# The second layer's up product by seven products of halves, with the three convolution taps made on ScalarE and added on VectorE one unit later

## The reference

```python
D_FF, CONV_W = 2816, 3

def conv_ffn(h, w_up, conv_w, conv_b, w_down):
    u = h @ w_up                                   # (1, 256, 1024) @ (1024, 5632)
    u = lax.conv_general_dilated(u, conv_w[:, None, :], window_strides=(1,),
                                 padding=[(CONV_W // 2, CONV_W // 2)],
                                 dimension_numbers=("NWC", "WIO", "NWC"),
                                 feature_group_count=u.shape[-1]) + conv_b
    a, g = jnp.split(u, 2, axis=-1)
    return (jax.nn.silu(g) * a) @ w_down
```

## Time and profile before

| | us |
|---|---|
| median of 3 runs | 3460.23 |
| lowest and highest | 3457.03, 3462.57 |
| the profiled execution, its whole time | 3458.15 |
| its span in the profile | 3456.3 |
| PE busy in it | 3286.9 (95%) |
| mean granted clock of PE | 0.964 of full speed |

### The profile page before, as it was taken

One profiled execution on the slowest core, in us unless ns is written; L12 is line 12 of the kernel. 1 busy time (PEld: TensorE's weight loads), 2 busy tenths in 40 slices (PEclk: granted clock), 3 DMA queues, 4 the chain that ended last, 5 costly groups with the idle time before them and its releaser, 6 DMA issues.

```text
span 3456.3 us, 81384 instructions
## 1 busy us (share of the span) xinstructions
PE 3286.9 (95%) x34930; PEld 2812.1 (81%) x34931; DVE 864.6 (25%) x1957; ACT 687.8 (20%) x1501; POOL 431.8 (12%) x393
## 2 busy tenths in 40 slices
PE   7999789999999999999999999988999999999998
PEld 5886678884587788787799887778899999988888
DVE  2324745550122321114233113130000100011001
ACT  2324132221113422112211021201111211110011
POOL 1210125550021010000057010000000000000000
PEclk9999689999999999999999999988999999999999
DMA  6546012222223244343344443237999999944477
GB/s 274 196 165 232 3 49 86 85 74 75 82 92 115 92 158 137 126 140 109 110 159 159 157 138 106 95 125 314 370 380 400 400 383 378 399 161 154 140 272 292
DMA packets 94776, 637.79 MB, mean 185 GB/s; under 512 B 10784, under 2 KB 11824, under 8 KB 38592
## 3 DMA queue, kind: packets, MB, share of 16 engines
q1 hardware_dynamic: 92048, 627.58, 48.8%
q0 software_dynamic: 2608, 8.49, 0.8%
HBM read 634.97 MB, written 1.05 MB: 184 GB/s over the span
## 4 chain that ended last, share of the span: by engine, by line
PE 89%; DMA 4%; DVE 3%; ACT 2%; issue 2%; POOL 0%; SPq 0%; DVEq 0%; ACTq 0%
PE bank L994 18%; PE bank L608 18%; PE bank L666 16%; PE bank L563 13%; PE bank L687 5%; PE bank L579 5%; DMA ring<-in_moe_down 3%; PE bank L954 2%; PE bank L511 2%; PE bank L537 1%; PE bank L1009 1%; PE bank L723 1%; PE bank L705 1%; PE bank L712 1%; DMA ring<-in_moe_up 1%
## 5 line engine op out<-in xcount | busy, mean ns | idle before, releaser
L666 PE MATMUL bank<-PROJ,ring 128*64 128x80 f32 (+2 forms) x7776 | 636.2, 272 | 11.9 <-DMA ring<-in_moe_down 8.8
L666 PEld LDWEIGHTS bank<-PROJ,ring 128*64 128x64 f32 (+1 forms) x7776 | 508.7, 147 | 137.6 <-issue 90.2
L994 PE MATMUL bank<-MIX,ring 128*64 128x80 f32 x12544 | 471.9, 234 | 19.8 <-issue 9.5
L994 PEld LDWEIGHTS bank<-MIX,ring 128*64 128x64 f32 x12544 | 446.6, 137 | 45.9 <-issue 38.3
L563 PE MATMUL bank<-H,ring 128*128 128x256 f32 x1856 | 408.2, 383 | 3.3 <-ACT H L1175 3.3
L563 PEld LDWEIGHTS bank<-H,ring 128*128 128x128 f32 x1856 | 355.0, 192 | 56.1 <-issue 4.7
L994 PE MATMUL bank<-H,ring 128*128 128x256 f32 x896 | 193.7, 379 | 0.0
L608 PE MATMUL bank<-H,ring 128*64 128x128 f32 (+1 forms) x1296 | 185.2, 331 | 5.5 <-ACT H L1175 4.8
L994 PEld LDWEIGHTS bank<-H,ring 128*128 128x128 f32 x896 | 170.2, 190 | 23.4 <-issue 0.3
L608 PE MATMUL bank<-MIX,ring 128*64 128x128 f32 (+1 forms) x1272 | 181.2, 321 | 0.8 <-DVE MIX L1748 0.8
L687 PE MATMUL bank<-H,ring 128*128 128x256 f32 x768 | 178.0, 389 | 3.9 <-ACT PROJ L1264 3.7
(11 more groups left out here) (345 smaller groups left out, 3440.8 us busy)
## 6 DMA issues: line engine op xcount, KB each, us to landing
ring<-in_moe_up SPq DMA_DIRECT2D x224, 1024.0 KB, 7.2
ring<-in_moe_down SPq DMA_DIRECT2D x128, 896.0 KB, 6.4
ring<-in_up SPq DMA_DIRECT2D x44, 1024.0 KB, 4.8
ring<-in_mod_b SPq DMA_DIRECT2D x40, 1024.0 KB, 5.6
ring<-in_tproj SPq DMA_DIRECT2D x32, 1024.0 KB, 4.9
ring<-in_proj SPq DMA_DIRECT2D x26, 1024.0 KB, 4.8
ring<-in_gates SPq DMA_DIRECT2D x24, 1024.0 KB, 4.8
ring<-in_down SPq DMA_DIRECT2D x32, 704.0 KB, 4.0
```

Source lines behind the costliest of these rows:

```text
L666: mm = pe.matmul(B[bank][lo:lo + m, 0:width], w[:, k, lo:lo + m], src(s * half + k), start=s == 0 and k == 0, stop=s == 1 and k == half - 1)
L994: mm = pe.matmul(B[(t0 + 2 * j + t) % 4][lo:lo + m, 0:n], w[:, k, t * P + lo:t * P + lo + m], src[:, k, 0:n], start=k == 0, stop=k == KT - 1)
```

## The change

`up1` is added to the table `SEVEN` with a width of 256. PE runs `seven("up1", ...)`: `seven_unit` for each of the 22 units in place of 16 plain products. The ring, the order of the loads and the down product stay.

- POOL: `w_sums` for units 0 and 1 when `wout1` is finished, then `sums_ahead` for each unit. It no longer multiplies `a` and `g` in `up1`.
- DVE: `x_sums` after the norm, `c_sums` for each unit. The outer taps are no longer scalar_tensor_tensor on PSUM but four tensor_tensor additions of finished taps (`add`, new lines 1852 and 1857), one unit late; the product of `a` and `g` (`gated`, new line 1862) comes here, two units late. All inputs of these five lie in SBUF.
- ACT: the copy of the first product; three taps for each of the two tiles, all read from Y (`taps`, new lines 1253 and 1255); Silu one unit late (new line 1261). The middle tap goes to SC, the outer ones to the right half of X, which is free in this layer.

```diff
-SEVEN = ('proj0', 'wout0', 'up0', 'proj1', 'swup')
+SEVEN = ('proj0', 'wout0', 'up0', 'proj1', 'up1', 'swup')
...
+        def tap(j, t, w):
+            return CONV[:, j % 2, t, 0:T] if w == 1 else X[:, 4 * (j % 2) + w + t, T:TC]
...
-            pairs("up1", T, ("norm6_out", 0, 1))
+            seven("up1", "norm6_out")
```

ScalarE, `conv_taps` (for each unit: `head(j + 1)`, which copies the first product, then `step_of(j)`):

```diff
+                def taps(j, it):
+                    act.wait_ge(S("ffn_hid"), it * NSLOT + (FT + j + 1))
+                    for t in range(2):
+                        src = flat(seven_parts("up1", j)[0][:, 2 * t:2 * t + 2, :])
+                        col = lambda w: cw[:, bass.ds(it * (4 * NSLOT) + 4 * (t * FT + j) + w, 1)]
+                        act.activation(tap(j, t, 1), src, ACT.Identity, bias=col(3), scale=col(1))
+                        for w in (0, 2):
+                            ins = act.activation(tap(j, t, w), src, ACT.Copy, scale=col(w))
+                    ins.then_inc(S("conv_c"), 1)
+
+                def silu(j, it):
+                    act.wait_ge(S("conv_d"), it * NSLOT + (FT + j + 1))
+                    g = tap(j, 1, 1)
+                    act.activation(g, g, ACT.Silu).then_inc(lin_free, 2)
+
+                def step_of(j, it):
+                    seven_done("up1", j, it)
+                    if j > 0:
+                        silu(j - 1, it)
+                    taps(j, it)
```

VectorE, `conv_taps`:

```diff
+                def add(j, it):
+                    dve.wait_ge(S("conv_c"), it * NSLOT + (FT + j + 1))
+                    for t in range(2):
+                        o = tap(j, t, 1)[:, 1:T]
+                        ins = dve.tensor_tensor(o, o, tap(j, t, 0)[:, 0:T - 1], ALU.add)
+                    ins.then_inc(S("conv_l"), 1)
+                    dve.wait_ge(S("conv_l"), it * NSLOT + (FT + j + 1))
+                    for t in range(2):
+                        o = tap(j, t, 1)[:, 0:T - 1]
+                        ins = dve.tensor_tensor(o, o, tap(j, t, 2)[:, 1:T], ALU.add)
+                    ins.then_inc(S("conv_d"), 1)
+
+                def gated(j, it):
+                    dve.wait_ge(lin_free, it * (2 * NSLOT) + (t0 + 2 * j + 2 + 4))
+                    dve.tensor_tensor(PROJ[:, bass.ds(it * (NSLOT * T) + j * T, T)], tap(j, 0, 1), tap(j, 1, 1), ALU.mult)\
+                       .then_inc(S("ffn_hid"), 1)
...
+                        c_sums("up1", j, it)
+                        add(j - 1, it)
+                        gated(j - 2, it)
...
+            x_sums("up1", "norm6_out")
```

GpSimd:

```diff
-            conv_ffn(1, T)
+            pool.wait_ge(unit_done, base["wout1"] + 4)
+            w_sums("up1", 0)
+            w_sums("up1", 1)
+            with pool.Fori(0, FT // NSLOT) as it:
+                for j in range(NSLOT):
+                    sums_ahead("up1", j, it)
```

More of the change, by code:

```diff
@@ L28 @@
 MOD_A = 8
-SEVEN = ('proj0', 'wout0', 'up0', 'proj1', 'swup')
-SEVEN_UNITS = {'proj0': 11, 'wout0': 4, 'up0': 22, 'proj1': 4, 'swup': 22}
-SEVEN_WIDTH = {'proj0': 512, 'wout0': 512, 'up0': 512, 'proj1': 512, 'swup': 256}
+SEVEN = ('proj0', 'wout0', 'up0', 'proj1', 'up1', 'swup')
+SEVEN_UNITS = {'proj0': 11, 'wout0': 4, 'up0': 22, 'proj1': 4, 'up1': 22, 'swup': 22}
+SEVEN_WIDTH = {'proj0': 512, 'wout0': 512, 'up0': 512, 'proj1': 512, 'up1': 256, 'swup': 256}
 MOD_P = 22
@@ L409, in seven_parts @@
             n, q = SEVEN_WIDTH[name] // 2, seven_at(name) + j
-            if name in ("up0", "swup"):
+            if name in ("up0", "up1", "swup"):
                 at = 6 * T * (q % 2)
@@ L1249, in conv_ffn, with conv_taps, head @@
                     pair(j, 0)
+            def conv_taps():
+                cw = W("conv1", 2 * FT * 4)
+                def head(j, it):
+                    seven_head("up1", j, it)
+                def taps(j, it):
[16 more added lines that the diff above has]
+                    taps(j, it)
+                peel = FT % NSLOT
+                head(0, 0)
+                for j in range(peel):
+                    head(j + 1, 0)
+                    step_of(j, 0)
+                with act.Fori(0, FT // NSLOT - 1) as it:
+                    for j in range(peel, peel + NSLOT):
+                        head(j + 1, it)
+                        step_of(j, it)
+                for j in range(FT - NSLOT, FT):
+                    if j + 1 < FT:
+                        head(j + 1, 0)
+                    step_of(j, 0)
+                silu(FT - 1, 0)
             def mod_row(n):
@@ L1818, in conv_ffn, with conv_taps @@
                     pair(j, 0)
+            def conv_taps():
+                t0 = tile_base["up1"]
+                def add(j, it):
[13 more added lines that the diff above has]
+                       .then_inc(S("ffn_hid"), 1)
+                peel = FT % NSLOT
+                for j in range(peel):
+                    c_sums("up1", j)
+                    if j > 0:
+                        add(j - 1, 0)
+                with dve.Fori(0, FT // NSLOT) as it:
+                    for j in range(peel, peel + NSLOT):
+                        c_sums("up1", j, it)
+                        add(j - 1, it)
+                        gated(j - 2, it)
+                add(FT - 1, 0)
+                gated(FT - 2, 0)
+                gated(FT - 1, 0)
             def causal_conv(l):
```

80 lines of the change are left out of this document (29 added, 51 removed).

## The result

The changed kernel takes 3477.47 us (median; 3476.23 to 3481.91), the kernel before in the same series 3458.84: a ratio of 1.0052, interval 1.0039 to 1.0065. The change makes it slower by half a per cent. The profiled execution took 3476.23 us with a span of 3474.4; that of before 3458.15 with 3456.3. So 18.1 us of span have to be found.

The account below looks back on a forecast made before the run. PE was taken to bound the kernel, but in `up1` the ACT and DVE round would become slower. Terms 2.5 + 3.0 + 7.8 + 2 = 15.3 on 3460.2 gave 3475.5 us, range 3453 to 3485.

Parts of the forecast that it names:

- The port: `up1`: DVE additions with two SBUF inputs wait for POOL, which holds the way about 1.14 of 1.27 us; they alternate.
- The round: `up1`: taps, additions, Silu, taps between ACT and DVE; 7.7 and 7.0 us with POOL's waits, mean 7.35, above PE's 6.11.
- the lag: `up1`: PE's slack before it waits for sums, up to 5.5 us, growing some 3 us a unit once begun.
- bare round: `up1`: taps 2.7, additions 1.5, Silu 0.42 and handing over, together 4.9 us without POOL, below PE's 6.11.
- 1, `up1`: `up1`: first unit 8.9 us, five units at 6.11, sixteen at 7.35; 157.1 for 154.6, so +2.5 us.
- 2, the norms: Norms ahead of `up1`: residual additions wait for POOL, one every 1.41 us instead of 0.67; +3.0 us.
- 3 and 4, the end and the clock: End of `up1`: PE waits +7.8 us at the first down tile's second half; lower clock after it, +2 (0 to 3).
- The term for the last tile: End of `up1`: additions, Silu, two further rounds and the last product bring the last hidden tile about 12.5 us after.
- 5, hidden things: First product's copy, `x_sums` and loads stay hidden; if ACT's register instructions show, round under 0.2 longer, end 2 us.
- PE stays last: `up1`: rival, waits under 1.2 us a unit keep PE's 6.11 pace; 3446 to 3450 us, chance 0.13.
- Cheap port: `up1`: rival, four additions pass POOL as one block, round 6.6 us; 3457.5 (3453 to 3467), chance 0.13.
- worse: `up1`: rival, all six taps at 0.50 us or clock falling in gaps of 1.2 us a unit; 3486 and more, chance 0.06.

Follow-up runs that it names:

- run 7: Changed kernel with ACT's four outer taps written to PSUM and `up1`'s products on banks 0 to 4: 3451.3 us, ratio 0.9974.
- run 1: Changed kernel with POOL's weight sums of units 2 to 21 of `up1` on 8 of their 512 columns: 3453.0 us, ratio 0.9975.
- Run 6: Changed kernel with POOL's weight sums of units 0 and 1 of `up1` made 21 us earlier: 3473.5 us, ratio 1.0038.
- Run 10: Changed kernel with first halves of two down tiles made before both second halves, no wait for Silu of unit 20: 3473.3 us, ratio 1.0042.
- run 5: Changed kernel with the padding ahead of the experts' loop jumped over and not run: 3464.5 us, ratio 1.0012.
- run 11: Kernel before the change with the padding ahead of the experts' loop jumped over: 3452.0 us, ratio 0.9981.
- Run 9: Changed kernel with POOL's weight sums of units 2 to 21 on 384 of their 512 columns: 3454.3 us, ratio 0.9990.
- run 3: Changed kernel with the four additions of a unit merged into two, both tiles in one instruction: 3473.1 us, ratio 1.0039.
- run 12: Changed kernel with outer taps in PSUM, early sums of units 0 and 1, padding jumped over, and new down-tile order: 3434.8 us, ratio 0.9927.
- run 8: Changed kernel with `up1`'s products on banks 0 to 4 and their two waits, taps still in SBUF: 3470.5 us, ratio 1.0031.

## Why the prediction was right, and where not

The forecast of 3475.5 was 2.0 low, and the mechanism is the one it names. But the term of the norms was too small, that of `up1` too large, the one of the end had the wrong place, and one term was missing. That the sum came so near is in part luck: the missing 3.5 us and the 1.0 of the norms were partly made up by 0.6 too much for `up1`, 0.6 too much for the end, and 0.5 that the rest of the program gave back.

**The port.** Right. Additions of 1.3 to 1.5 beside POOL, 0.42 alone, and 0.42 again with one input in PSUM (run 7). The Trainium skill, SBUF — State Buffer, section "Who interferes with whom", was the rule behind it, and runs 1 and 7 bear out both of its halves, the contention of two SBUF inputs (1048 ns beside POOL's full sums, 428 beside its short ones) and the free way of a PSUM one (414). What the trace adds is that DVE's queued instructions let POOL in between.

**The round.** Right, and 0.05 too long: 7.30 for 7.35, as 6.82 and 7.7 to 7.8 in turn (7.0 and 7.7 forecast). That the lag grows by some 3 us a unit once it has begun stood there without a working; it came so, 3.4 and 2.9 in the rounds of 9.54 and 9.04, since the product waited as well. Waits of 3.0 and 2.05 us in the two kinds of unit, by L1852 and L1857, for 2.8 and 2.1. The pieces of the bare round hold as well: Copy every 0.40, Identity every 0.49, and at the end of `up1`, where POOL is idle, sums come 4.70 apart for my 4.9.

**1, `up1`.** +1.9 for +2.5. The first unit, five at 6.11 and then PE waiting is how it went (first wait at 1236.4). From there to the last product it is 117.1 us for the 117.6 of sixteen rounds. The term was 0.6 too large, nearly all of it there.

**2, the norms.** +4.0 for +3.0, mis-sized. L1613 comes every 1.41 as worked out, but I let PE's means be only one chunk behind; the last three chunks' means ran together, 2.72 us from 1189.73, at a granted clock of 0.50. Run 6 shows the cause and the size.

**3 and 4, the end and the clock.** +9.2 for 7.8 + 2 = 9.8. The sum is right, its place isn't. The gap is not at the second half of the first down tile but ahead of its first product: that tile waits for Silu of unit 20 (through `lin_free`), which began 5.8 us after the last product (1357.66; the row names DVE, whose product had just ended). 6.3 us there, then the first half at half clock (+2.9), and by its end the last hidden tile was there. The term for the last tile, 12.5 us behind the last product, measured 11.3. Run 10 took the gap apart.

**5, hidden things.** They were hidden; the six register instructions a unit don't show. But the step failed in one place: it looked for what the change adds to engines and queues, and not at PE's program. +3.5 us came 1000 us later, where padding instructions are run: +4.7 there and -1.2 in the wait behind them. With the padding jumped over, both kernels take 10.1 us for that stretch (runs 5 and 11).

**The rivals.** "PE stays last" was said to need waits under one POOL instruction a unit. Run 9 bears that out nearly: with three quarters of POOL's time the waits are 1.2 and 1.4 us a unit (1.94 and 2.18 for 0.76), and the round is at PE's pace. It also shows how near that case was: at most a quarter of POOL's time away. "Cheap port" is refuted by the changed kernel itself, where two queued additions took 2.78 us with a wait for each, and by run 3: even merged additions waited, and the product behind them, too. Of "worse" neither half came: the outer taps run every 0.40, and the clock stayed at 1.00 through PE's waits of 0.5 to 1.5 us (window 1204 to 1346).

The parts sum to 15.3 in the forecast and to 18.1 in the trace; the medians differ by 17.2 to 18.6, by which earlier median one takes.

## What to carry to other kernels

Before work moves to VectorE beside a busy GpSimd, count its instructions with two SBUF inputs and step the round through: each can wait for a whole GpSimd instruction. If one input can be left in PSUM (free banks, or fewer for the products), the same work costs its bare time: here that turned a ratio of 1.0052 into 0.9974. And where a round of two engines lies close to the pace of the third, ask where it falls under that pace, not for the proportion: below it nothing is lost.

## What the runs showed of the hardware that I had not expected

- Padding ahead of an aligned loop costs PE time: 10.10 us after the change, 5.39 before, none with a jump over it (runs 5, 11, 12). The runs with PE's program of the change stand at 10.0 to 10.3, so what moved it was the other program for `up1`. That the padding instructions are run one by one is what the jump's gain says; their number was not read.
- Even with the jump, 2.55 us of "issue" are left at the branch past the full-width path (3.48 to 4.95 with padding). The Trainium skill, Runtime: NRT & Kernel Launch, section "Instruction fetch mechanics", says that a taken branch to code outside the two pages held makes the engine wait for a fetch. It gives no time; that these 2.55 us are such a fetch no run here shows.
- The loss at the port isn't in proportion: POOL sums of 1.27 us give units of 7.30, sums of 1.00 give 6.11, as sums of 0.2 to 0.4 do.
- The granted clock in the 5 us behind PE's gap at the end of `up1`, by run: gap 2.5 us, clock 1.00 (runs 1 and 7); 3.0, 1.00 (run 10); 3.3, 0.66 (run 9); 4.3, 0.51 (run 8); 5.8, 0.55 (run 3); 6.3, 0.50 (the changed kernel). A shorter lag of the round so shortens the gap and, in runs 1, 7 and 10, keeps the clock behind it.
